# Matmul operands walked from the last column to the first: the split products of a three-block transformer kernel

## The reference, cut to what matters

```python
# first block, layer 0: gated short convolution;  layer 1: latent attention
b, c, h = jnp.split(x_n @ w_in, 3, axis=-1)
return (b * causal_dwconv(c * h, conv_w)) @ w_out
# after each of them, and once more in the second block
g, u = jnp.split(causal_dwconv(x_n @ w_up, conv_w), 2, axis=-1)     # 1024 -> 5632
return (jax.nn.silu(g) * u) @ w_down                                 # 2816 -> 1024
# second block: proj = h @ w_in, three mixers, then @ w_out, then the same kind of FFN
```

## Time and profile before

| | |
|---|---|
| median of 2 runs | 1749.38 us (1749.15 to 1749.61) |
| span of the profiled execution, first to last instruction | 1748.3 us |
| instructions | 21957 |
| TensorE matmul records | 7845 |
| busy share PE, DVE, ACT, POOL | 99%, 65%, 39%, 22% |
| mean granted TensorE clock | 0.996 of full |
| HBM traffic | 106 GB/s over the span |

### The profile page before, as it was taken

The page is one execution under the profiler, slowest core; times in us unless marked ns, Lnnn a source line. Parts: engine busy times, 40 slices in busy tenths (PEclk is TensorE's granted clock), DMA queues, the critical chain, the costliest instruction groups (busy, mean ns, idle before and its releaser), DMA issues.

```text
span 1748.3 us, 21957 instructions
## 1 busy us (share of the span) xinstructions
PE 1723.8 (99%) x7845; PEld 1393.1 (80%) x7845; DVE 1136.2 (65%) x1428; ACT 679.8 (39%) x919; POOL 393.1 (22%) x169
## 2 busy tenths in 40 slices
PE   9999999999999999999999999999999999999998
PEld 6888788888887876878888888888657788888886
DVE  7566777776656886677777676563765677777222
ACT  4123444444333335444444422432563544444221
POOL 2444100000544330210000055444202200000442
PEclk9999999999999999999999999999999999999999
DMA  5233232233664220132222366332201232222232
GB/s 196 97 108 98 91 99 96 98 96 112 226 216 145 97 85 1 61 108 96 96 96 96 122 218 213 137 107 85 72 1 49 77 103 96 96 96 96 97 109 72
DMA packets 52188, 186.34 MB, mean 107 GB/s; under 512 B 5920, under 2 KB 6048, under 8 KB 52128
## 3 DMA queue, kind: packets, MB, share of 16 engines
q1 hardware_dynamic: 51552, 184.34, 31.6%
q10 hardware_dynamic: 576, 1.20, 0.2%
HBM read 183.41 MB, written 2.10 MB: 106 GB/s over the span
## 4 chain that ended last, share of the span: by engine, by line
PE 91%; DVE 5%; ACT 3%; issue 1%; POOL 0%; DMA 0%; DVEq 0%; ACTq 0%; SPq 0%
PE ps L1528 27%; PE ps L1530 27%; PE ps L1529 27%; PE ps L1828 1%; PE ps L1798 1%; PE ps L1713 1%; PE ps L1715 1%; PE ps L1714 1%; DVE RAB L1105 1%; PE ps L1805 1%; DVE acc L907 1%; PE ps L1817 1%; PE ps L1573 0%; PE ps L1939 0%; PE ps L1587 0%
## 5 line engine op out<-in xcount | busy, mean ns | idle before, releaser
L509 POOL TENSOR_TENSOR WL<-raw,WH 128x1024 fp32r<-128x1024 f32 x156 | 382.0, 2449 | 1320.6 <-ACT WH L554 1320.6
L1528 PE MATMUL ps<-XH,WH 128*128 128x512 f32 x1480 | 579.4, 392 | 1.9 <-POOL XL L516 0.9
L1530 PE MATMUL ps<-XH,WL 128*128 128x512 f32 x1480 | 576.0, 389 | 0.0
L1529 PE MATMUL ps<-XL,WH 128*128 128x512 f32 x1480 | 575.9, 389 | 0.0
L554 ACT ACTIVATE WH<-raw 128x1024 fp32r<-128x1024 f32 x291 | 308.4, 1060 | 571.9 <-PE ps L1530 534.0
L1528 PEld LDWEIGHTS ps<-XH,WH 128*128 128x128 f32 x1480 | 277.9, 188 | 63.8 <-issue 2.5
L1530 PEld LDWEIGHTS ps<-XH,WL 128*128 128x128 f32 x1480 | 277.8, 188 | 58.2
L1529 PEld LDWEIGHTS ps<-XL,WH 128*128 128x128 f32 x1480 | 277.9, 188 | 58.0 <-issue 1.0
L1528 PE MATMUL ps<-HH,WH 128*128 128x512 f32 x528 | 205.5, 389 | 0.0
L1529 PE MATMUL ps<-HL,WH 128*128 128x512 f32 x528 | 205.4, 389 | 0.0
L1530 PE MATMUL ps<-HH,WL 128*128 128x512 f32 x528 | 205.4, 389 | 0.0
(11 more groups left out here) (280 smaller groups left out, 1958.0 us busy)
## 6 DMA issues: line engine op xcount, KB each, us to landing
raw<-w_tiles SPq DMA_DIRECT2D x291, 512.0 KB, 3.3
ada<-ada_tiles SPq DMA_DIRECT2D x32, 512.0 KB, 5.6
trig<-ada_tiles SPq DMA_DIRECT2D x16, 512.0 KB, 6.9
X<-x_in SPq DMA_DIRECT2D x4, 512.0 KB, 6.3
out_x<-X SPq DMA_DIRECT2D x8, 256.0 KB, 2.0
RAB<-c_in SPq DMA_DIRECT2D x2, 512.0 KB, 4.6
MK<-mask_in ACTq DMA_DIRECT2D x1, 640.0 KB, 3.8
trig<-rope_in SPq DMA_DIRECT2D x2, 256.0 KB, 2.9
```

Source lines behind the costliest of these rows:

```text
L509: nc.gpsimd.tensor_tensor(WL[k % SPL][:, :], raw[:, k, :], f32(WH[k % SPL][:, :]), ALU.subtract).then_inc(s_lo, 1)
L1528: mm(bank, h, xh, start=first, stop=False)
L1529: mm(bank, h, xl, start=False, stop=False)
L1530: return mm(bank, lo, xh, start=False, stop=last)
```

## The change

`dot` makes reversed views of the bank and of both halves of the moving operand, and uses them in all its three matmuls. The weight block, the order of the matmuls, the flags, the waits, the buffers and the signals are as before. Column j of the moving operand still meets column j of the bank, so each value is computed from the same terms; only the order in which the 512 columns pass is turned round. `token_dot`, `first_tile`, `low_last` and all other matmuls keep their order.

```diff
--- before.py
+++ after.py
@@ -1525,9 +1525,10 @@
 
                 h = WH[t % SPL][:, blk * P:(blk + 1) * P]
                 lo = WL[t % SPL][:, blk * P:(blk + 1) * P]
-                mm(bank, h, xh, start=first, stop=False)
-                mm(bank, h, xl, start=False, stop=False)
-                return mm(bank, lo, xh, start=False, stop=last)
+                back, xh, xl = bank[:, ::-1], xh[:, ::-1], xl[:, ::-1]
+                mm(back, h, xh, start=first, stop=False)
+                mm(back, h, xl, start=False, stop=False)
+                return mm(back, lo, xh, start=False, stop=last)
 
             def wide(t, M, i=0, per=0, before=None, src=(XH, XL), ready=True, within=None):
 
```

## The result

| | before | after |
|---|---|---|
| median | 1749.38 us | 1789.12 us |
| span of the profiled execution | 1748.3 us | 1787.0 us |
| ratio of the times | | 1.0225, 95% interval 1.0208 to 1.0243 |

The account below looks back on a forecast made before the run. PE, busy 1723.8 of 1748.3 us, was taken to bound the kernel. Zero for instructions, backward read and backward write left the median, 1749.4 us, as forecast; the range was 1740 to 3150 us.

Parts of the forecast that it names:

- The bound and the count: PE bounds the whole kernel; `dot` has 6552 matmuls without cover, so one nanosecond more per matmul adds 6.55 us.
- Part 1: Instructions, waits, signals and DMAs of the changed kernel: none added, removed or moved; cost 0, gain 0.
- Part 3: Writing the bank backwards in `dot`: taken as 0, though no matmul in the trace tested it.
- Part 2: Reading the moving operand backwards in `dot`: taken as 0, since a descending row touches the same neighbouring words.
- case A: No effect in `dot`: one column per clock in either direction, 1749.4 us, own range 1745 to 1757; chance 0.60.
- Four runs of 64: Trace row of a moving operand in four 64-column runs, 0.843 ns a column against 0.836 unbroken: breaks claimed free.
- Rival B: Half pace in `dot`: descending columns lose paired access, 0.428 to 0.440 us per matmul, 3068 to 3147 us; chance 0.24.
- five cases: Outcomes for `dot`: no effect 0.60, half pace 0.24, start-up cost 0.12, gain 0.02, worse than half pace 0.02.
- Rival C: Start-up cost: each reversed `dot` matmul pays 13.4 ns once more, +88 us, so 1837 us; chance 0.12.
- every-fourth rows: Trace rows of matmuls taking every fourth column, 0.234 us per 128 columns against 0.122 contiguous: a factor of about two.
- The rule weighed against the row: Skill's rule that non-contiguous PSUM patterns slow matmuls; strictly read about +1319 us for `dot`, by 8-byte lines 0.
- the sign named for case C: `dot` matmuls 0.24 us from start to start, while plain 32-bit lines 1568, 1828 and 1968 keep their distances.

Follow-up runs that it names:

- the third probe: Kernel before plus 26 groups of 24 matmuls behind its computation, varying weight block place, width and operand type; upward read 233.3 ns with the block at column 16.

## Why the prediction was right or wrong

- *The bound and the count* held: PE is on the path all the way, 6552 matmuls of `dot`, no cover, 6.55 us per nanosecond.
- *Part 1*, instructions and waits at 0: right. The counts are the same.
- *Part 3*, the bank at 0: right, and shown apart from the rest by the run with the write alone (1.0002).
- *Part 2*, the moving read at 0: this is the step that failed. It measured 6.6 ns per matmul, 43.2 us by the pace and 39.7 us in the medians, and that made the likeliest case A wrong: 1789 us against its own 1745 to 1757, and just over the 2%. The argument "a descending row touches the same neighbouring words" is refuted as it stands: runs of 16 columns upwards touch the same words and pay as well. For rows read upwards, what counts is their place against the weight block whose load runs beside them, modulo 64 columns. That the reversed row loses by the same meeting fits every run and is not shown by one of its own. Four runs of 64 in an unbroken order could not show it: they are plain 32-bit, which the third probe found blind to direction, and they keep the sequence.
- *The range*, 1740 to 3150 us, holds the 1789, by luck. Its upper bound was put there to reach B, whose mechanism did not happen, and none of the five cases had this size: it lies between the 1757 of A and the 1837 of C.
- *Rival B*, half pace: wrong. It would have shown 428 to 440 ns apart, it is 233.3. Nor do the every-fourth rows bear on it. B's weight of 0.24 was too high and made the upper bound of the range far too wide.
- *Rival C*, some nanoseconds for each matmul, was the nearest in size (88 us against 40) but not in kind. It is no start-up cost paid once by every reversed matmul: it is absent in 256 columns, and an upward read can have such a price too. It had 0.12 and should have had the most among the slower cases. A price of a few nanoseconds has only 5.3 ns to pass before it decides, and nothing in the trace bounded it from above at less.
- *The rule weighed against the row.* Writing a bank downwards gave 1.0002. The Trainium skill (PSUM — Partial Sum Buffer, Specifications) says that any non-contiguous pattern slows matmuls significantly; read as any pattern but step +1, it does not hold here, and the measurement decides. Its looser reading, by lines of 8 bytes, agrees with this run, which does not test it further.
- *What would show it*: the sign named for case C, a distance above 0.227 us with the plain 32-bit lines unchanged (line 1828, now 1829: records of 275 ns in both kernels), is what the trace shows, at 0.233 instead of 0.240.

## What to carry to other kernels

With `float32r` operands at full pace and 512 columns, keep each moving row and the weight block at the same place modulo 256 bytes, and walk the row upwards; falling runs of 64, 128 or 256 columns were free too. Off that, a matmul took 229.2 to 235.8 ns in the probes instead of 226.7, up to 4% more. Writing the bank downwards was free (1.0002). When PE is 99% busy, ask of every edit to `dot` what a few nanoseconds times its count would make, before asking about factors of two.

## What the runs showed of the hardware

- For `float32r` the weight load is not independent of the moving read. Moving nothing but the weight block by 16 columns took a matmul from 226.7 to 233.3 ns. The Trainium skill (TensorE: Matmul & The Clock Gate, Step-by-step: what each phase is for) says that loading the next weights does not steal read bandwidth from the running matmul, since there are two read ports. For `float32r` these runs don't agree that the two are independent; for 16-bit and plain 32-bit operands no run moved the weight block, so they don't show it.
- The period is 64 columns, 256 bytes. The Trainium skill (SBUF — State Buffer, Specifications) names lines of 16 bytes; places 16 bytes apart do differ (226.7 ns at column 0, 231.7 at 4), but no unit of 16 bytes explains that column 16 still costs and column 64 does not. What lies behind this period is open.
- Read upwards from an aligned place, a `float32r` matmul has 13 to 14 ns beside its columns at 256 (119.6 ns, 106.7 of them columns), 384 (173.8 and 160.0) and 512 columns (226.7 and 213.3), but 16.7 at 480 (216.7 and 200.0). 16-bit operands have about 163 ns at 384 (3.92 / 24), 3 beside theirs. No form of 512 `float32r` columns went below 226.7 ns, so none of these runs beats the kernel before.
